# Memory stage of a hybrid encoder layer: x loaded behind three weight units, unit 0 split within the memory norm, x's upper parts on VectorE

## The reference

```
m   = rmsnorm(mem, mem_norm)               # 256 memory tokens
mk  = m @ xattn_wk ; mv = m @ xattn_wv     # keys and values of the memory, two outputs
x   = x + 0.5 * swiglu(rmsnorm(x, ffn1_norm)) ...
...                                        # attention, delta rule, merge, cross attention, FFN 2, final norm
rmsnorm(x, g) = x * rsqrt(mean(x*x) + 1e-6) * g
```

## Time and profile before

| | us |
|---|---|
| median of 3 runs | 3374.44 |
| lowest, highest | 3370.88, 3379.51 |
| the profiled execution: its time | 3380.14 |
| its span, first to last instruction | 3378.3 |
| its mean granted clock of TensorE | 0.989 |

### The profile page before, as it was taken

How to read it: one execution, slowest core, us unless ns; L and a number is a source line. 1 busy time by engine, 2 the same in 40 slices (tenths; PEclk the granted TensorE clock), 3 DMA queues, 4 the chain that set the end, 5 groups by cost and what they waited for, 6 DMA issues and landing times.

```text
span 3378.3 us, 50143 instructions
## 1 busy us (share of the span) xinstructions
PE 3241.6 (96%) x19977; PEld 3080.8 (91%) x19977; DVE 1320.8 (39%) x2297; ACT 679.8 (20%) x1326; POOL 957.9 (28%) x436
## 2 busy tenths in 40 slices
PE   6899999999999999999999999999899999999998
PEld 5899999999978888888887989988799999999997
DVE  2233233233356645653342466232325232333324
ACT  5100000000133333433433242133311000000001
POOL 3533333333322222211112033221133333333341
PEclk9999999999999999999999999999999999999999
DMA  5411111111142233211112145024311111111111
GB/s 193 139 38 37 50 43 42 39 43 43 42 163 76 95 128 136 78 41 68 60 53 74 41 162 176 19 100 157 126 34 49 44 43 43 43 37 43 37 44 63
DMA packets 93338, 248.70 MB, mean 74 GB/s; under 512 B 11664, under 2 KB 50320, under 8 KB 90512
## 3 DMA queue, kind: packets, MB, share of 16 engines
q1 hardware_dynamic: 48640, 154.09, 13.6%
q10 hardware_dynamic: 44560, 92.60, 7.5%
HBM read 197.87 MB, written 48.79 MB: 73 GB/s over the span
## 4 chain that ended last, share of the span: by engine, by line
PE 86%; DVE 6%; issue 3%; ACT 2%; DMA 1%; POOL 1%; ACTq 1%; DVEq 0%; POOLq 0%
PE psum L164 60%; PE psum L260 12%; DVE n_tmp L557 1%; PE psum L1796 1%; PE psum L1732 1%; PE psum L939 1%; PE psum L2763 1%; PE psum L1009 1%; PE psum L2736 1%; POOL w_lo L2271 1%; PE psum L984 1%; DVE a_sc L1333 1%; PE psum L1746 1%; PE psum L1740 1%; PE psum L2742 1%
## 5 line engine op out<-in xcount | busy, mean ns | idle before, releaser
L131 POOL TENSOR_TENSOR w_hi<-w_raw,zero 128x1024 fp32r<-128x1024 f32 x199 | 383.6, 1928 | 2114.0 <-PE psum L164 1321.5
L164 PE MATMUL psum<-x_hi,w_hi 128*128 128x384 f32 x2928 | 573.3, 335 | 17.2 <-issue 4.2
L164 PE MATMUL psum<-x_lo,w_hi 128*128 128x384 f32 x2928 | 574.6, 336 | 0.0
L164 PE MATMUL psum<-x_hi,w_lo 128*128 128x384 f32 x2928 | 570.0, 334 | 0.0
L164 PEld LDWEIGHTS psum<-x_hi,w_hi 128*128 128x128 f32 x2928 | 511.4, 188 | 26.3 <-issue 11.1
L164 PEld LDWEIGHTS psum<-x_lo,w_hi 128*128 128x128 f32 x2928 | 515.6, 189 | 2.4 <-issue 0.9
L164 PEld LDWEIGHTS psum<-x_hi,w_lo 128*128 128x128 f32 x2928 | 513.4, 188 | 0.0
L134 POOL TENSOR_TENSOR w_lo<-w_raw,w_hi 128x1024 fp32r<-128x1024 f32 x199 | 494.1, 2483 | 15.6
L419 DVE TENSOR_TENSOR f_hid<-psum,f_gate 128x384 f32<-128x384 f32 x132 | 73.6, 558 | 858.8 <-PE psum L164 856.4
L366 ACT ACTIVATE f_gate<-psum 128x384 f32<-128x384 f32 x132 | 64.8, 493 | 1478.2 <-PE psum L164 1474.5
L164 PE MATMUL psum<-f_h_hi,w_hi 128*128 128x384 f32 x1056 | 269.5, 336 | 0.0
(11 more groups left out here) (303 smaller groups left out, 3386.2 us busy)
## 6 DMA issues: line engine op xcount, KB each, us to landing
w_raw<-units SPq DMA_DIRECT2D x224, 512.0 KB, 3.5
gate_dram<-b_stash ACTq DMA_DIRECT2D x48, 192.0 KB, 1.9
e_gate<-gate_dram ACTq DMA_DIRECT2D x48, 192.0 KB, 2.6
a_kc<-k_cache ACTq DMA_DIRECT2D x4, 2048.0 KB, 7.6
a_vc<-v_cache ACTq DMA_DIRECT2D x4, 2048.0 KB, 12.8
proj_dram<-a_cv ACTq DMA_DIRECT2D x12, 576.0 KB, 2.7
b_pad<-proj_dram SPq DMA_DIRECT2D x12, 576.0 KB, 4.8
x_sk<-mem_k ACTq DMA_DIRECT2D x6, 1024.0 KB, 7.3
```

The lines of the kernel that those rows point to most:

```text
L131: pool.tensor_tensor(k.w_hi[s][:, :], k.w_raw[s][:, :], k.zero[:, 0:1].to_broadcast([P, D]), ALU.add)\
L164: mm = pe.matmul(out, wl if part == 2 else wh, (xl if part == 1 else xh)[:, n0:n1], start=(part == 0 and i == 0), stop=(part == 2 and i == ...
```

## The change

Three things are changed in the memory stage.

1. SP issues the load of x behind those of weight units 0, 1 and 2 (`then` is called by `load_units` behind its third load), not ahead of them.
2. ScalarE makes the upper part of unit 0 between the memory norm's root and that norm's own upper parts, and the upper part of unit 1 after these. Only then does it wait for x.
3. The six upper parts of x are made by VectorE (`upper_on_vector`, a `tensor_copy` of the same shape), between its scaling and its lower parts of the same third. ScalarE's turns 5, 7 and 9 keep the root alone.

```diff
+    def upper_on_vector(self, dve, n):
+        s = self.s
+        for h in range(2):
+            c = slice(4 * h, 4 * h + 4)
+            dve.wait_ge(s.nscaled.sem, s.nscaled.at(2 * n + h + 1))
+            dve.tensor_copy(self.hi[:, c, self.cols(n)], self.tmp[:, n % 2, c, :]).then_inc(s.nhi.sem, 1)
...
-                5: [lambda act: norm.root(act, 0), lambda act: norm.upper(act, 0)], 6: [lambda act: norm.gather(act, 1)],
-                7: [lambda act: norm.root(act, 1), lambda act: norm.upper(act, 1)], 8: [lambda act: norm.gather(act, 2)],
-                9: [lambda act: norm.root(act, 2), lambda act: norm.upper(act, 2)]}
+                5: [lambda act: norm.root(act, 0)], 6: [lambda act: norm.gather(act, 1)],
+                7: [lambda act: norm.root(act, 1)], 8: [lambda act: norm.gather(act, 2)],
+                9: [lambda act: norm.root(act, 2)]}
...
-        load_units(sp, k, k.next_unit, 1, UNITS)
+        load_units(sp, k, k.next_unit, 1, UNITS,
+                   then=lambda: sp.dma_start(norm.x[:], by_frame(k.xt)).then_inc(k.x_loaded.sem, 16))
...
-        own_norm.scalar(act)
+        act.preload_act_table_set("natural_log_exp_and_others")
+        own_norm.square(act, 0)
+        own_norm.gather(act, 0)
+        own_norm.root(act, 0)
+        unit_upper(0)
+        own_norm.upper(act, 0)
+        unit_upper(1)
         act.wait_ge(k.x_loaded.sem, k.x_loaded.at(16))
-        for j in range(2):
-            unit_upper(j)
...
-        norm.vector(dve, both=True)
+        for n in range(norm.nb):
+            norm.scale(dve, n)
+            norm.upper_on_vector(dve, n)
+            norm.lower_both(dve, n)
...
-                sp.dma_start(x_early[:], by_frame(k.xt)).then_inc(k.x_loaded.sem, 16)
```

## The result

The changed kernel takes 3382.69 us in the median of 20 runs (3371.82 to 3388.97), the kernel before 3377.89 us beside it (3370.88 to 3384.12). The ratio is **1.0015, with a 95% interval of 1.0008 to 1.0021**: 2.7 to 7.1 us slower, 5.1 in the middle. The forecast was +5.1 us, with 0.73 on a change of less than about 0.3%.

The account below looks back on a forecast made before the run. VectorE and GpSimd, working in series, were taken to bound the changed memory stage: first FFN product +3.9, cold product +2.2, bias table -1.0, sum +5.1 us against the profiled execution. Against the median: 3379.5 us, range 3364 to 3388.

Parts of the forecast that it names:

- slower and not 17 to 20 us faster: Memory stage: from ScalarE alone a gain of 17 to 20 us; with VectorE and GpSimd in series, +5.1 us instead.
- The start: Start of the memory stage: memory norm unchanged, unit 0 split earlier, first product at about 20.8 instead of 23.6.
- The landing of x: Load of x behind three weight units: lands at 26, just hidden by products 0 and 1; bounds 0 to 2 us.
- The series: From x's first root: 53.2 + 28.4 + 19.0 + 12.8 = 113.4, less 2.8 overlap; x's split ends at 110.6, 3.9 later.
- the rule of the Trainium skill: VectorE and GpSimd: the first to issue holds the shared ports for its whole instruction; no overlap, split ends at 113.4.
- the 0.2 us for each operation of GpSimd: VectorE and GpSimd in series: each hand-over to GpSimd overlaps 0.2 us; 14 operations, 2.8 us.
- Behind it: After the split of x: cold first FFN product +2.2 us, bias table landing sooner -1.0 us.
- The first (no hindrance): Rival: VectorE and GpSimd hardly hinder each other; first FFN product at 86 to 97, about 3359 us; chance 0.13.
- The second: Rival: ScalarE and late stores still pace the memory stage; first FFN product at 102 to 105, about 3371; chance 0.10.
- The third (slow copies): Rival: full exclusion and copies of 1.71 us; split of x ends at 118.5, about 3388 us; chance 0.09.
- the fourth (late x): Rival: x lands at 29 instead of 26, total +8, 3382 us; counted within the likeliest case's 0.68.
- The two traces should differ by a constant: After the first FFN product: traces before and after differ by a constant; a growing difference would make the reading wrong.

Follow-up runs that it names:

- Experiment 2: Kernel before with part 3 alone: VectorE makes the upper parts of x, loads and units 0 and 1 as before; ratio 1.0015 to the kernel before.
- experiment 1: Kernel before with parts 1 and 2 alone, ScalarE keeping the upper parts of x; ratio 0.9993 to the kernel before.
- experiment 3: Changed kernel, with GpSimd waiting for the whole split of x before it takes FFN units 0, 1 and 2; ratio 1.0002 to the kernel before.
- experiment 4: Changed kernel with the reciprocal roots of the memory norm and x's norm in PSUM instead of SBUF; ratio 0.9962 to the kernel before, median 3365.55 us.
- experiment 6: Changed kernel with only the memory norm's root in PSUM, that of x's norm staying in SBUF; ratio 1.0018 to the kernel before.
- experiment 8: Kernel before with both roots in PSUM and nothing else changed; ratio 0.9995 to the kernel before.
- second profiled execution of the changed kernel: The changed kernel run once more, unchanged, as a single execution; 3386.46 us, first FFN product at 111.90.

## Why the prediction was right, step by step

**That the change is slower and not 17 to 20 us faster: right, and for the reason given.** VectorE and GpSimd work in series from the first root on, and the first FFN product waits for VectorE. Experiment 2 shows that part 3 alone brings the loss, experiments 1 and 3 show it gone or mostly gone with VectorE's copies or GpSimd's FFN units taken away, and experiment 4 shows the cause by removing the shared input alone. That +5.1 is also the middle of the measured interval is partly luck: the terms below are off by up to 1.3 us each, in both directions.

**The start: wrong by 2.1 us.** The step "the memory norm doesn't change ... So the first product starts at about 20.8" failed; it was 22.86. I applied the exclusion to x's norm and not to the memory norm, where unit 0's earlier split puts a GpSimd operation beside the scalings. Experiments 4 and 6, with first products at 20.58 and 20.63, show that this is all of it. The landing of x (predicted 26, ScalarE released at 26.12) was right.

**The series: right in its terms.** First scaling at 54.5 (predicted 53.2). It is only 1.3 us late and not 2.1, mostly because the 24 matmuls of the first memory product happened to take 4.2 us (22.86 to 27.06) instead of the 5.3 us of the trace before; experiment 8 had 4.2 us with the order of before, so this is no gain of the change. 54.5 + 28.4 + 19.0 + 12.8 = 114.7; it ended at 111.29, so the overlaps were 3.4 us instead of 2.8. The copy of 128x1536 takes 0.9 us undisturbed (1.81 for two), against 0.86 in the prediction; its own 0.53 ns an element gives 0.81. By the rule of the Trainium skill that the prediction names (SBUF — State Buffer, Who interferes with whom), without overlap, it would have been 114.7. Taking something off was right, but the 0.2 us for each operation of GpSimd was a choice: in the same rows VectorE lost 3.8 us to two operations of GpSimd that take 4.5 us, which is an overlap of 0.36 us each and would have taken off 5.0. The changed kernel shows 3.4 / 14 = 0.24 us. The first FFN product came 4.66 us later than before, where 3.9 was predicted; the series began 1.3 us later and overlapped 0.6 more.

**Behind it: right in sign, both sizes off.** The cold first FFN product took 117.18 - 111.39 = 5.79 us, against 4.38 in experiment 4 (97.81 - 93.43), where TensorE came to it without a long pause: +1.4, not +2.2. In the second profiled execution of the changed kernel it took 118.82 - 111.90 = 6.92 us, +2.5, so the 2.2 lies between the two. The granted clock was 0.57 in 88 to 107 and 0.80 in 107 to 126. The bias table landed 6.0 us after its issue instead of 9.1 (118.31 to 124.32), which took the whole wait of 2.32 us off the fifth job, not 1.0. So the terms were +4.66 + 1.4 - 2.3 = +3.8, and the mark moved by +3.56, where +5.1 had been predicted; in the second execution it moved by 131.42 - 126.22 = +5.20. The kernel before has one trace only, so a part of either number is its own scatter. The ratio's interval of 2.7 to 7.1 us holds all of them.

**The rivals.** The first (no hindrance) is out. The second was wrong for the changed kernel in both profiled executions, but its order of work came up in experiment 6 by another way: FFN units 1 and 2 behind x's split, not because stores are late but because VectorE got the turns, and without the time of 3371 (3378.27). The third (slow copies) is out by the row at 106.14, the fourth (late x) by ScalarE's release at 26.12. "The two traces should differ by a constant" after the first FFN product was wrong: what lies behind varies between executions of any kernel here.

**Open:** what decides in an execution whether GpSimd gets its turn between VectorE's copies and lower parts or waits for all four. I saw both with one program, and made no experiment that sets it. It isn't settled once for an execution either: in that of experiment 4 the GpSimd operation at 57.90, beside a first copy, took 6.97 us and waited for two copies and two lower parts, while the one at 80.21, beside the last third's copies, took 2.50 us and ran between them. By line L2283, from experiment 4 and from experiment 6:

```profile
L2283 POOL TENSOR_TENSOR w_lo<-w_raw,w_hi x1: 6972/6972/6972, 57.9 to 57.9; 128x1024 fp32r<-128x1024 f32 x1
...
L2283 POOL TENSOR_TENSOR w_lo<-w_raw,w_hi x1: 7159/7159/7159, 74.1 to 74.1; 128x1024 fp32r<-128x1024 f32 x1
```

## What to carry to other kernels

When a stall is removed, list what the stalled engines did not do at the time, and what will now run beside it: here ScalarE's wait had kept GpSimd quiet while VectorE worked, and taking it away put 28 us of VectorE and 32 us of GpSimd in series. Look elsewhere in the same trace for the same operations side by side; one row of 8.12 us against 4.33 gave the price. The remedy was an input's place, a root in PSUM instead of SBUF, which turned +5 us into -13 us without one instruction more; it is worth nothing where nothing runs beside it.

## What the hardware showed that I had not expected

One program took turns between VectorE and GpSimd in two ways. In one, GpSimd got in between VectorE's instructions: it was late by 0.1 to 0.3 us beside scalings and by up to 1.5 beside lower parts (3.41 instead of 1.89), and eight scalings with four operations of GpSimd beside them took 12.9 us. In the other, VectorE's two copies and two lower parts ran in 1.8 and 3.4 us without a gap, GpSimd waited through all of them (7.16 instead of 2.38 us), and eight scalings, with three operations beside them, took 10.65. And a store of 128 KB that ScalarE issues can land late beside weight loads: in the changed kernel the one issued at 38.33, with no weight load on its way, took 1.7 us to its landing, the one at 78.35, behind two loads issued at 77.08 and 77.45, took 4.6. The evacuations waited for stores nine times, 11.3 us in total, in the changed kernel, against five times and 9.5 us before.
